# First modulation weights in two feature halves, second group in six buffers, x statistics by token: one core, 1024-wide two-layer hybrid decoder step

## What is computed

```python
sh1, sc1, g1, sh2, sc2, g2 = split(silu(c) @ w_ada[layer] + b_ada[layer], 6)
h = rms_norm(x, norm_g[layer, 0]) * (1 + sc1) + sh1
q, k, v, bg, cg, xin = split(h @ w_in_ab, ...)          # layer 0
attn = moba(q, k, v, cache_k, cache_v, page_table)      # sample: 8 pages of 128 rows per row of the batch
mix = concat([attn, bg * short_conv(cg * xin)]) @ w_out_ab
u, v = split(h @ w_in_c, 2)                             # layer 1
mix = (u * (w_s @ rms_norm(v) + b_s)) @ w_out_c
x = x + g1 * mix
h = rms_norm(x, norm_g[layer, 1]) * (1 + sc2) + sh2
x = x + g2 * (square(relu(h @ w_ff1[layer])) @ w_ff2[layer])
y = rms_norm(x, g_final)
```

## Time and profile before

| | us |
|---|---|
| median of three runs | 1422.98 |
| lowest, highest | 1417.11, 1423.3 |
| the profiled execution's own time | 1417.6 |
| its span | 1415.9 |
| TensorE busy | 1349.5 (95%) |
| VectorE, ScalarE, GpSimd busy | 618.7, 449.9, 162.3 |
| mean granted TensorE clock | 0.989 of full |
| moved by DMA | 191.47 MB, mean 135 GB/s |

### The profile page before, as it was taken

How to read it: one execution, slowest core, us unless ns; L and a number is a source line. 1 busy time by engine, 2 the same in 40 slices (tenths; PEclk the granted TensorE clock), 3 DMA queues, 4 the chain that set the end, 5 groups by cost and what they waited for, 6 DMA issues and landing times.

```text
span 1415.9 us, 26167 instructions
## 1 busy us (share of the span) xinstructions
PE 1349.5 (95%) x10436; PEld 1245.5 (88%) x10436; DVE 618.7 (44%) x1093; ACT 449.9 (32%) x743; POOL 162.3 (11%) x204
## 2 busy tenths in 40 slices
PE   5889999999989999999999999999999999999996
PEld 2668877667878998998999999899999999999996
DVE  2523422554345333333334564566666343443432
ACT  2523321443334213213213331323344331321332
POOL 3200000681231000000000120002103000000000
PEclk9899999999999999999999999999999999999998
DMA  9587688320546526426322223122222322222211
GB/s 352 180 318 223 207 284 279 127 90 30 194 164 224 172 91 232 151 89 234 134 86 89 90 68 112 34 90 90 60 90 90 104 89 90 89 89 89 78 42 64
DMA packets 125546, 191.47 MB, mean 135 GB/s; under 512 B 5692, under 2 KB 100425, under 8 KB 119316
## 3 DMA queue, kind: packets, MB, share of 16 engines
q1 hardware_dynamic: 117060, 135.41, 29.6%
q0 software_dynamic: 8400, 54.86, 10.7%
HBM read 185.63 MB, written 4.62 MB: 134 GB/s over the span
## 4 chain that ended last, share of the span: by engine, by line
PE 90%; DMA 3%; ACT 2%; DVE 2%; issue 1%; POOL 1%; SPq 1%; DVEq 0%; POOLq 0%; ACTq 0%
PE gemm L1402 76%; PE aux_ps L1437 2%; PE gemm L1526 2%; PE stat_ps L1714 1%; DMA raw_panels<-in_w_in_ab 1%; PE stat_ps L1538 1%; PE aux_ps L1575 1%; PE gemm L1678 1%; DMA xs_tok<-in_x_sample 1%; DMA kv_ring<-in_cache_v 1%; PE gemm L1486 1%; POOL ssq L410 1%; SPq L330 0%; POOL hf L421 0%; PE aux_ps L1678 0%
## 5 line engine op out<-in xcount | busy, mean ns | idle before, releaser
L1402 PE MATMUL gemm<-h_split,w_hi 128*128 128x272 f32 (+1 forms) x3584 | 614.3, 294 | 12.9 <-DVE h_split L971 9.3
L1402 PEld LDWEIGHTS gemm<-h_split,w_hi 128*128 128x128 f32 x3584 | 509.0, 190 | 52.3 <-issue 48.6
L1402 PE MATMUL gemm<-hid_split,w_hi 128*128 128x272 f32 x2304 | 384.1, 288 | 1.4 <-issue 1.0
L1402 PE MATMUL gemm<-h_split,w_lo 128*128 128x272 f32 (+1 forms) x1792 | 374.1, 290 | 0.0
L1402 PEld LDWEIGHTS gemm<-hid_split,w_hi 128*128 128x128 f32 x2304 | 325.7, 188 | 1.9 <-issue 1.8
L549 ACT ACTIVATE w_hi<-raw_panels 128x1024 fp32r<-128x1024 f32 x184 | 193.5, 1052 | 333.9 <-PE gemm L1402 319.5
L1402 PEld LDWEIGHTS gemm<-h_split,w_lo 128*128 128x128 f32 x1792 | 284.4, 189 | 0.0
L902 DVE TENSOR_TENSOR w_lo<-raw_panels,w_hi 128x1024 fp32r<-128x1024 f32 x184 | 227.6, 1237 | 112.3 <-ACT w_hi L549 110.9
L1402 PE MATMUL gemm<-hid_split,w_lo 128*128 128x272 f32 x1152 | 238.2, 288 | 0.0
L1402 PEld LDWEIGHTS gemm<-hid_split,w_lo 128*128 128x128 f32 x1152 | 180.3, 188 | 0.0
L916 DVE SCALAR_TENSOR_TENSOR ffv<-gemm,rel 128x544 f32<-128x544 f32 x56 | 40.6, 724 | 201.6 <-ACT rel L569 201.6
(11 more groups left out here) (252 smaller groups left out, 824.2 us busy)
## 6 DMA issues: line engine op xcount, KB each, us to landing
raw_panels<-in_w_ff SPq DMA_DIRECT2D x64, 1024.0 KB, 5.3
ada_w<-in_w_ada POOLq DMA_DIRECT2D x42, 1024.0 KB, 5.3
kv_ring<-in_cache_k SPq DMA_DIRECT2D x64, 256.0 KB, 3.3
kv_ring<-in_cache_v SPq DMA_DIRECT2D x64, 256.0 KB, 4.1
raw_panels<-in_w_in_ab SPq DMA_DIRECT2D x12, 1024.0 KB, 8.1
raw_panels<-in_w_in_c SPq DMA_DIRECT2D x8, 1024.0 KB, 5.3
ada_early_h<-in_w_ada POOLq DMA_DIRECT2D x4, 1024.0 KB, 18.1
raw_panels<-in_w_out_ab SPq DMA_DIRECT2D x4, 1024.0 KB, 5.1
```

What stands on the lines that cost most here:

```text
L1402: ins = mm(G[slot][:, 512 - T0W * (1 - half):512 + (T0W + rows) * half], w[:, s, k, :], rhs[:, k, part, T0W * half:T0W + (T0W + rows) * half],
```

## The change

**Statistics by token.** ScalarE squares the rows of `x_tok` with a running sum (five instructions), takes logarithm and exponential on five columns; VectorE multiplies the identity with them (`x_diag`), TensorE multiplies ones with these diagonals, which puts 1/rms of every token on all partitions, and ScalarE copies it to `rstd`. x is copied 544 wide by VectorE alone. TensorE runs 64 turns of the identity into a free bank before it waits for x.

**First group in halves.** Sixteen DMAs of 512 KB (per partition two pieces of 512 numbers: shift and scale of the same features) instead of eight of 1024 KB. `half_products(0)` and `half_turn(0)` serve h's chunks 0 to 3; the second half's products and turn stand inside the pair ahead of its chunk 4, and VectorE splits unit 2's weights there.

**Second group.** It is now parts 2 and 4 (gate 1 and scale 2) and has six buffers (`ada_e` twice, `ada_w` twice, `ada_v0` twice); seven chunks stand before page unit 4 and one behind it. The third group is parts 3 and 5.

**V pages** are loaded by POOL, four at a time, with semaphores `vq_in`; the quads lie at other places: (0,0) and (0,1) after units 10 and 11, the others inside units 12 to 17, up to three in a unit. The turn of the convolution state moves into unit 17.

**Attention.** The banks `TMB` rotate over four; a half unit stands before the first scores; `HALF_AT` and `COPY_AT` shift, and ScalarE copies P ahead of the outcome of a unit.

**Norm 1** now works as norms 2 and 3 do, and the split of the mixer's outcome goes into buffers of its own (`mix_hi`, `mix_lo`), since `h_split` receives y at that time. h of norms 1 and 3 is made beside the first four units of `down(0)`, two chunks a unit.

**Layer 1.** `v_turn` 0 to 4 stand inside two units; T_OUTC runs as single units.

```diff
-        HALF_AT = {0: (2,), 1: (3,), 2: (4, 5), 3: (6,), 4: (7,), 5: (8, 9), 6: (10, 11)}
-        COPY_AT = {0: 18, 2: 19, 3: 20, 5: 21, 6: 22}
...
+        HALF_AT = {0: (3,), 1: (4,), 2: (5,), 3: (6, 7), 4: (8,), 5: (9,), 6: (10, 11)}
+        COPY_AT = {0: 19, 2: 20, 3: 21, 5: 22}
...
-            sp.wait_ge(ada0_in[6], 16)
+            sp.wait_ge(ada0_in[5], 32)
...
-            v_pages(0, 10)
...
             pool.wait_ge(c_in, 48)
-            for k in range(KC):
-                pool.dma_start(ADA0[k], ada_v[0][0, :, k, :]).then_inc(ada0_in[k], 16)
-            for m in range(1, 7):
-                add_squares(norm[0], m)
...
+            for half in range(2):
+                for k in range(KC):
+                    pool.dma_start(ADA0[half][k].rearrange("p (s n) -> p s n", s=2),
+                                   ada_col[:, k, 0:2, half, :]).then_inc(ada0_in[4 * half + k // 2], 16)
...
+            load_first(0)
+            load_first(1)
+            norm_apply(0, range(4))
+            pool.wait_ge(ada_used, 8)
+            for k in range(2, 6):
+                load_first(k)
+            norm_apply(0, range(4, KC))
...
+                for i in range(4):
+                    pool.wait_ge(page_free, pos + i + 1)
+                    pool.dma_start(kv_ring[:, (pos + i) % 8, :],
...
+            for tt in range(5):
+                m, src = (128, x_tok[:, tt, :]) if tt < 4 else (32, xs_tok[:, :])
+                if tt:
+                    act.wait_ge(x_sq, tt)
+                A(x_junk[0:m, :], src, ACT.Square, accum_out=x_ss[0:m, 0, tt:tt + 1]).then_inc(x_sq, 1)
...
+                        V.tensor_scalar(x_diag[:, tt, :], ident[:, :], x_ss[:, 2, tt:tt + 1], None, ALU.mult).then_inc(x_dg, 1)
...
+            for _ in range(64):
+                tr(ST[:, 1, 128:256], ident[:, :], ident[:, :])
             pe.wait_ge(x_in, 80)
...
+            half_products(0, range(4))
+            pe.wait_ge(x_dg, 5)
+            for tt in range(4):
+                mm(ST[:, 0, 128 * tt:128 * tt + 128], ones[:, :], x_diag[:, tt, :], start=True, stop=True)
...
-            pair(0, hn, from_norm(0))
-            ada_chunk(1, 0)
-            ada_chunk(1, 1)
-            unit(0, 2, hn)
...
+            pair(0, of(hn), first_rows)
+            first_chunk(0)
+            first_chunk(1)
+            unit(0, 2, of(hn))
...
+            unit(3, 3, of(hn), at(k0=quad(1, 0), k3=quad(1, 1), k6=quad(1, 2)), slot=0)
             turn_o(0)
...
+            unit(4, 0, of(hn), at(k0=quad(1, 3), k3=quad(1, 4), k6=quad(1, 5)), slot=0)
+            unit(4, 1, of(hn), at(k0=quad(1, 6), k1=turn_state, k4=quad(1, 7), k5=lambda: own_values(1)), slot=0)
...
+            pe.wait_ge(tmb_ev, 8)
+            half_unit(2)
...
-                if layer == 0:
-                    with_ada(3, T0, hn, from_norm(nn), at=((0, 1), (), (2,), (3,), (4, 5), (6,), (7,)))
-                else:
-                    early_unit(T0, nn)
-                    for s in range(1, 8):
-                        unit(q0 + s // 4, s % 4, hn, rows=NROW + 1)
+                early_unit(T0, nn)
+                for s in range(1, 8):
+                    if layer == 0:
+                        ada_chunk(3, s - 1)
+                        if s == 7:
+                            ada_chunk(3, 7)
+                    unit(q0 + s // 4, s % 4, of(hn), rows=NROW + 1)
...
-            pair(T_OUTC // 4, hid, gated_rdy)
-            for s in range(2, 8):
-                unit(T_OUTC // 4 + s // 4, s % 4, hid)
+            for s in range(8):
+                unit(T_OUTC // 4 + s // 4, s % 4, of(hid), None if s else gated_rdy)
```

548 lines of the change are left out of this document (320 added, 228 removed).

## The result

The changed kernel takes 1405.12 us, median of four runs (1404.13 to 1406.98); the kernel before took 1423.14 beside it (1417.11 to 1425.87). The ratio is 0.9881, with a 95% interval of 0.985 to 0.9912: faster, by 1.2%. The prediction, 1387 with a range of 1375 to 1402, had the sign right and the size wrong by nearly a factor of two.

What follows compares the result with a forecast made beforehand. It took TensorE, busy 1349.5 of 1415.9 us, as the bound. The terms summed to -33.0 on the profiled 1417.6, giving 1384.6, or 1390.0 on the median; it took the middle, 1387, range 1375 to 1402.

Steps and rivals of the forecast that it cites:

- What bounds the kernel: Whole kernel: TensorE busy 1349.5 of 1415.9 us, so gains must come from 66.4 us of idle time or low-clock work.
- Term 1: Start and second group: first product at 31.3, page units at 75.0 instead of 87.84, -12.8 us.
- Term 2: K and V pages: removed waits and low clock save 6.8 us, POOL's page loads add 8.0, net +1.2.
- Terms 3 and 4: Token banks and conv state, -3.6 us; attention, -5.3 us: waits go and the low clock behind them.
- Term 5: First MLP norm: raw y goes in and h is made beside down(0), 59.8 us instead of 66.5, -6.7.
- Term 6: Layer 1: turns of v inside units, T_OUTC in single units, last norm's h in four units, -4.8 us.
- (b): V pages: POOL's page period is the worse one, +11 us against the forecast, 1398; chance 0.12.
- (c): Start: the 64 idle turns ahead of x cost more than they give, first product ten us later, 1397; chance 0.15.
- (a): V pages: the stage costs nothing new since page loads run ahead, 8 us less, 1379; chance 0.10.
- (d): Start: the weight halves come no earlier, the first landing near 33, 1394; chance 0.05.
- (e): V pages: POOL's quad period dominates all sixteen quads, slower than before, about 1430 at 8 us a quad; chance 0.03.
- The queue's latency: V pages on POOL: first byte about 1 us on the software queue, 0.6 on hardware, about 3 us worse.

Runs made afterwards that it cites:

- half1_late_split: Changed kernel with second half's products right behind the first half's turn, their turn before the pair's fourth chunk, unit 2's panel split after h's sixth chunk: 1402.25 us.
- v_on_sp: Changed kernel with V pages issued by SP instead of POOL, quads staying at the new places: 1401.94 us, ratio 0.9892.

## Why the prediction was wrong, point by point

**What bounds the kernel** was right: the gain came from idle time, 12.1 us less, with TensorE's busy time up by 1.2. From the low clock nothing came on the whole (mean 0.989 before, 0.987 after): attention won some of it and the pages lost some.

**Term 1, start, forecast -12.8, measured -4.9.** The landing of half 0 was no bound: its products began at 23.09, behind x. The failing steps: "the first half's products end 0.5 after the weights" took them as paced by the DMA, where TensorE does them serially in 1.93 + 1.93; the hole was taken over from before with two steps halved, without asking what ScalarE does first (a panel that lands at 28.13); and the second half, "products are done at 41.5", were costed by their landing at 41.1, when they cost 3.8 us of TensorE from 44.53 on. A fourth term, the copy-out ahead of the first page unit (1.66), was put at nothing. The rest was near: four chunks took 8.6 us (8.4 forecast), the hole at the fifth 6.1 from the end of the products at 48.2 (6.1 forecast), the last four 8.0 (8.4). half1_late_split shows that 5.3 of the 7.9 us lost at the start are order. The first product is another matter: whatever the order it came no earlier than 35.47. As the rows read, the two splits of panel 0 (2.0 us of ScalarE, 2.4 of VectorE) lie between that panel's landing at 28.1 and the product wherever they stand, and the forecast's hole of 5.1 had no place for them. The 15% allowed for smaller pieces is shown by no run: the engines moved 376 to 384 GB/s from 13.5 to 28.3 us, against 389 from 5 to 25 before. The six buffers did their part: no wait for second-group weights is left.

**Term 2, pages, +1.2 forecast, +15.2 measured (14.2 with the chunk that moved).** The period was right where it shows: two of POOL's quads start 3.99 us apart, 2.32 of issues and 1.66 of registers, against the 4.2 assumed. That the waits in the second group sum to 1.66 + 0.58 + 3.00 + 1.34 = 6.6 us, against 6.5, is luck in good part: there are four unequal waits in place of seven of 0.9, the other quads of POOL start when TensorE frees a slot, and with SP as issuer at the same places 8.0 us of waits were left in both groups together. The two longest waits for pages end with pages that took 7 us to land, where the median is 4.6 (chain that ended last, start and length):

```profile
186.25 7.02 DMA kv_ring<-in_cache_v
...
240.64 7.10 DMA kv_ring<-in_cache_v
```

SP had issued a raw panel of 1024 KB 2.3 us before each (at 184.00 and 238.29), and the DMA engines were full then (374 GB/s from 185.7 to 189.4). Such slow pages occur with either issuer (6.2 us in v_on_sp); that the panel slows them is a guess that no run tested. What the forecast missed besides stands around the second group: in the first group 1.95 + 2.40 + 0.89 (a K page) instead of 1.5; a wait of 1.2 for VectorE's copy of `kT_pages`; the held bank, 3.72, which the order of VectorE's instructions showed and which I had not followed; and the clock, counted as a gain where waits went and not as a cost where they came (0.55 of full over 6.6 us, 0.71 over 3.7, some 4 us). The change put waits of 1.95, 2.40, 3.72 and 3.00 in the place of the removed ones. That the new stalls came near the upper bound of 19.3 is luck too: the bound was made from a period of 5.1 to 5.2 us a quad, which did not come.

**Terms 3 and 4, -8.9 forecast, -9.9 measured.** Right. Idle time fell from 7.8 to 2.0 us and TensorE's busy time from 105.4 to 101.3, the granted clock rose from 0.97 to 1.00. No wait of the earlier trace rows in the banks or at the half units is left; a wait of 1.54 ahead of P's turn at 273.54, which the forecast did not count, went too; two of 0.72 and 0.63 stand at the first heads, and the 0.69 ahead of the last values stayed.

**Term 5, -6.7 forecast, -5.5 measured (-4.6 with the 0.9 by which the way there grew).** From the statistics' place to the first down block it took 61.0 us (412.07 to 473.05) where I had 59.8; before, 66.5. T_OUT itself grew by 1.3, of which 0.69 is a wait for a weight chunk and the rest the group's turn, which now stands inside it. The forecast's parts add up to 59.6, not 59.8, and the 15% of 4.2 MB in term 1 would be 1.6 to 1.9 us, not 1.1: slips too small to matter. The steps beside down(0) cost nothing: from there to the MLP's last unit both kernels took 359.45 us. The chain's step answers to the earlier trace rows:

```profile
473.05 48.22 PE gemm L1512 x384
```

```profile
382.89 1.07 PE L1547 MATMUL aux_ps<-ada_w,cT 128*32 128x512 f32 x8 [0.69 <-DMA ada_w<-in_w_ada]
```

**Term 6, -4.8 forecast, -5.7 measured.** Right. The wait of 2.04 in the earlier trace rows is 0.50 now, T_OUTC starts without the 1.00 that it had waited before, and a chain step shows TensorE running through the places of the others:

```profile
1003.82 347.39 PE gemm L1512 x2754
```

**The rivals.** (b), a worse POOL period, gave 1398 with a chance of 0.12, and had the right stage but a reason that the period of 3.99 does not bear out. (c) was refuted: with the turns, x ran at 0.60 to 0.66 a group. (a), (d) and (e) did not come true. What happened was the sum of several small misses of one sign, which no single rival held; the range, made of single rivals, was too narrow for it. **The queue's latency**: the sentence on the first byte of the software queue pointed the right way (at the old places a V page landed in 4.1 us from POOL and 3.9 from SP), but of POOL's price of 4.6 to 6.5 us most went with the register reads, as far as one pair of traces shows.

**Still open**: why executions of one kernel differ by 3 to 9 us with the same work; and what made page loads take 7 us. The price of the T_OUTC and v_turn edits apart was not tried either.

## What to carry to other kernels

Cost a moved step on its engine, not by its data: what comes when must be read down the list of each engine that touches it, and an in-order engine that holds a PSUM bank behind an unrelated copy stalls as surely as a late DMA. A ring of two quads was tight here with either issuer once the quads stood some 3.5 us apart (229.17 and 232.63 in the changed kernel): set their distance against freeing a slot, register reading, issues and the slowest landing, not the median one, before moving loads to another engine. When a change makes new holes of 2 to 4 us on TensorE, allow for the low clock behind them, as one would subtract it for the holes that go, but as a range: of four such holes here two were followed by it. And read the scatter of the landmarks off kernels that share a stage before calling 1 or 3 us a gain.
